# One decoder block with 32 experts: TensorE's order of work within an expert, and when the selection table is made

## The chip, the cores and the metric

One core of a Trainium2 chip runs the whole block in one program. The metric is the device time of one execution in microseconds (us); of several runs the median counts.

## The reference, cut to what matters

The program computes one decoder layer for 256 tokens of width 1024: a state-space branch and an attention branch over projections of the normalised input, a cross-attention into 256 memory tokens, a mixture of experts and a last normalisation. The change lies in the mixture of experts. Each token goes to 4 of 32 experts:

```python
logits = hf @ w_router + b_router
top_v, top_i = lax.top_k(logits, TOP_K)          # TOP_K = 4 of 32
gate = jax.nn.softmax(top_v, axis=-1)
# for the tokens xb of expert e:
gu = xb @ w_gu[e] + b_gu[e]                      # (tokens, 2048)
g_lin = jnp.minimum(gu[..., :D_FF], 7.0)
u_lin = jnp.clip(gu[..., D_FF:], -7.0, 7.0)
act = g_lin * jax.nn.sigmoid(1.702 * g_lin) * (u_lin + 1.0)
yb = act @ w_down[e] + b_down[e]                 # D_FF = 1024
y[token] += gate * yb
```

All is float32. The experts' weights are 32 x (8 MB + 4 MB).

## The kernel before, in words

Every engine has an instruction list of its own, written out by hand, and semaphores order the lists against one another. A `wait_ge(sem, n)` in a list stops that engine's queue until the semaphore is at n; what stands behind it waits too. The first part (to about 393 us) is the two branches, the cross-attention and the router. Then come the experts, in the function `experts` of each engine: a loop of 4 turns (`Fori(0, NIT)`) over a body of 8 experts (`BODY`), written out. The experts are taken in groups of 4 (`GE`), with 64 token slots an expert (`SLOTS`). If an expert had more than 64 tokens, further passes would run; here none does.

**Weights.** SP (L369 to L388) issues the transfers: for each expert 8 chunks of 1 MB of `w_gu` and 4 of `w_down` (`EXP_CH` = 12), into a ring of 16 slots (`RING_MOE`; 12 in `ring`, the rest in the buffers `small`, `xn`, `gates` and `kv`, free by then). SP issues chunk m when TensorE has used chunk m - 16, which the semaphore `chunk_used` counts. TensorE waits for a chunk on `slot_full`. This wait and the ring are the only thing that paces the transfers.

**One expert on TensorE** (L798 to L849), in this order:
- bias (L809): four 32-row products of the selection table `sel` (32 partitions, 4 experts x 64 slots, ones in the row of the expert) with `b_gu`, which open the sums in PSUM banks 4 and 5;
- gate/up (L818): 8 chunks x 4 products onto the same banks, `chunk_used` after each chunk;
- combine (L794): the down products of the expert before, copied by VectorE to `yb`, are added into banks 0 to 3 at their tokens through the table `hotT`; it waits for `yb_ready`;
- gather (L768): a quarter of the tokens of the next group of four experts is picked with the one-hot table `onehot`, into bank 7. After four experts the next group's tokens are all there (`xgT`, two buffers);
- transposes of this expert's gate table (L827, into bank 6), and, when VectorE has taken the gathered block (`gather_out`) and made the activation (`act_ready`), of the activation (L834, into bank 7);
- down (L845), when ScalarE has copied both transposes out (`ht_out`, `at_out`): 4 chunks, onto bank 6.

A product of a 64-slot expert is written twice, for the two halves of its columns, into the upper and lower 64 partitions of a bank. Each instruction of this float32 form shows twice in the trace.

**One expert on VectorE** (L1425 to L1462): minimum and clip of gate and up (L1448, L1449, the second sets `gu_read`), two products for the activation (L1452, L1456, `act_ready`), taking the gathered block (L1404 in `take_gathered`, `gather_out`), copying the down products to `yb` (L1462, `yb_ready`). At every fourth expert (`j % GE == 0`) VectorE does ahead of this: the gate table of the group (L1434, two instructions), `sel` for the group (L1441; it waits until the gate/up products of the expert before are done), and the one-hot for the next group (L1396 in `next_onehot`, `hot_ready`). **ScalarE** (L1066 to L1074): the sigmoid, and the two copies out of PSUM.

At a group's start TensorE waits ahead of the bias products for `hot_ready`:

```python
if j % GE == 0:
    pe.wait_ge(hot_ready, it * 2 + (j // GE + 2))
    pe.wait_ge(gather_out, it * 8 + (4 * (j // GE) + 4))
```

That `sel` is ready is told by `hot_ready`, since VectorE makes the one-hot after it.

Of the kernel before, what the change touches and what calls it, by code (L numbers as in the profile page):

```python
# [27 lines left out]
KD = D // P  # L28
# [8 lines left out]
NE, TOPK, FF = 32, 4, 1024  # L37
# [15 lines left out]
SLOTS = 64  # L53
GE = 4
# [5 lines left out]
EXP_CH = KD + FF // P // 2  # L60
# [30 lines left out]
FRONT_CH = len(CHUNKS)  # L91
# [48 lines left out]
STEP_CH = BODY * EXP_CH  # L140
# [18 lines left out]
def build(nc, x, mem, g_mix, w_in, conv_w, conv_b, dt_bias, a_log, d_skip, g_ssd, w_ssd_out,  # L159
# [5 lines left out]
    with ctx:  # L165
# [40 lines left out]
        identx = sb("identx", [NE, TABW])  # L206
# [56 lines left out]
        bgu = xcf[0:NE, 0:2 * FF]  # L263
# [15 lines left out]
        sel = scr[0:NE, 3, 0:GE * SLOTS].rearrange("p (e s) -> p e s", e=GE)  # L279
# [3 lines left out]
        def ring_slot(m):  # L283
# [4 lines left out]
        ps = ctx.enter_context(nc.psum_tensor("ps", [P, 8, 512], F32))  # L288
# [34 lines left out]
        gl_ready, gu_read, sg_ready, act_ready = map(  # L323
            sem, ("gl_ready", "gu_read", "sg_ready", "act_ready"))
        ht_done, ht_out, at_done, at_out, yb_ready, comb_done, y_done, yb_last, up_ready, h_full, \
            gatehot_made = map(
            sem, ("ht_done", "ht_out", "at_done", "at_out", "yb_ready", "comb_done", "y_done",
                  "yb_last", "up_ready", "h_full", "gatehot_made"))
        dve_step, act_step = sem("dve_step"), sem("act_step")
        out_sem, out_ready = sem("out_sem"), sem("out_ready")  # L330

# [136 lines left out]
        def _(pe):  # L468
# [295 lines left out]
            def gather(k0, bank=7):  # L764

                for k in range(2):
                    for b in range(TB):
                        i = mm(ps[:, bank, k * T:(k + 1) * T], hn2[:, b, (k0 + k) * P:(k0 + k + 1) * P],  # L768
                               onehot[:, b, :, :].rearrange("p e s -> p (e s)"), start=(b == 0), stop=(b == 1))
                i.then_inc(gathered, 1)  # L770
# [16 lines left out]
            def combine(done=comb_done, each=False):  # L787
# [7 lines left out]
                               skip_group_check=True)  # L795
                i.then_inc(done, 1)

            def experts(it):  # L798


                for j in range(BODY):
                    n = it * BODY + j
                    xg = xgT[j // GE]
                    if j % GE == 0:
                        pe.wait_ge(hot_ready, it * 2 + (j // GE + 2))
                        pe.wait_ge(gather_out, it * 8 + (4 * (j // GE) + 4))
                    for q in range(2):
                        for half in range(2):
                            mm(ps[64 * half:64 * half + 64, 4 + q, :], sel[:, j % GE, :],  # L809
                               bgu[:, q * FF + half * 512:q * FF + half * 512 + 512],  # L810
                               start=True, stop=False, skip_group_check=True)
                    for k in range(KD):
                        m = FRONT_CH + j * EXP_CH + k
                        pe.wait_ge(slot_full[slot(m)], it * (16 * STEP_CH // RING_MOE) + filled(m))
                        w = ring_slot(m)
                        for q in range(2):
                            for half in range(2):
                                i = mm(ps[64 * half:64 * half + 64, 4 + q, :],  # L818
                                       xg[:, k, (j % GE) * SLOTS:(j % GE + 1) * SLOTS],
                                       w[:, q * FF + half * 512:q * FF + half * 512 + 512],  # L820
                                       start=False, stop=(k == KD - 1), skip_group_check=True)
                        i.then_inc(chunk_used, 1)
                    pe.wait_ge(yb_ready, n + 1)
                    combine()
                    gather(2 * (j % GE))
                    for b in range(TB):
                        i = nc.tensor.transpose(ps[:, 6, b * P:(b + 1) * P],  # L827
                                                gatehot[:, b, j % GE].rearrange("p u s -> p (u s)"),
                                                ident[:])
                    i.then_inc(ht_done, 1)  # L830
                    pe.wait_ge(gather_out, it * 8 + (j + 5))
                    pe.wait_ge(act_ready, n + 1)
                    for c in range(4):
                        i = nc.tensor.transpose(ps[:, 7, c * P:(c + 1) * P], actv[:, c * P:(c + 1) * P], ident[:])  # L834
                    i.then_inc(at_done, 1)
                    pe.wait_ge(ht_out, n + 1)
                    pe.wait_ge(at_out, n + 1)
                    for k in range(FF // P):
                        m = FRONT_CH + j * EXP_CH + KD + k // 2
                        if k % 2 == 0:  # L840
                            pe.wait_ge(slot_full[slot(m)], it * (16 * STEP_CH // RING_MOE) + filled(m))
                        w = ring_slot(m).rearrange("p (k n) -> p k n", k=2)
                        fh, c = k // 4, k % 4
                        for half in range(2):
                            i = mm(ps[64 * half:64 * half + 64, 6, :], actT[:, c, fh * 64:fh * 64 + 64],  # L845
                                   w[:, k % 2, half * 512:(half + 1) * 512],
                                   start=(k == 0), stop=(k == FF // P - 1), skip_group_check=True)
                        if k % 2:
                            i.then_inc(chunk_used, 1)  # L849
# [239 lines left out]
        def _(dve):  # L1089
            V = nc.vector  # L1090
            count = [0]

            def step(ins):

                count[0] += 1
                ins.then_inc(dve_step, 1)
                dve.wait_ge(dve_step, count[0])
# [304 lines left out]
            def take_gathered(buf, k0, bank=7):  # L1402
                g = pcol[:, ROW_MOE + k0:ROW_MOE + k0 + 2].unsqueeze(2).broadcast_to([P, 2, T])
                V.tensor_tensor(buf[:, k0:k0 + 2, :], ps[:, bank, :].rearrange("p (k s) -> p k s", k=2), g,  # L1404
                                ALU.mult).then_inc(gather_out, 1)
# [7 lines left out]
            for p_ in range(NPASS):  # L1413
# [2 lines left out]
                    step(V.tensor_scalar(rankx[:, :, c], r0, -float(SLOTS * p_), None, ALU.add))  # L1416
                step(V.tensor_copy(gatex[:, :, c], gate_d[:]))

            step(V.memset(hotT, 0.0))
            V.memset(yb, 0.0).then_inc(yb_ready, 1)  # L1420
            for k0 in range(0, KD, 2):
# [3 lines left out]
            def experts(it):  # L1425
                for j in range(BODY):
                    n = it * BODY + j
                    if j % GE == 0:
                        gr = it * 2 + j // GE


                        dve.wait_ge(hot_ready, it * 2 + (j // GE + 1))
                        for b in range(TB):
                            i = V.tensor_tensor(gatehot[:, b],  # L1434
                                            onehot[:, b].unsqueeze(2).broadcast_to([P, GE, 2, SLOTS]),
                                            gatex[:, b, bass.ds(gr * GE, GE)].unsqueeze(2).unsqueeze(2)
                                            .broadcast_to([P, GE, 2, SLOTS]), ALU.mult)
                        i.then_inc(gatehot_made, 1)

                        dve.wait_ge(chunk_used, it * STEP_CH + (FRONT_CH + (j - 1) * EXP_CH + KD))  # L1440
                        V.tensor_copy(sel, identx[:, bass.ds(gr * GE, GE)].unsqueeze(2).broadcast_to([NE, GE, SLOTS]))  # L1441

                        dve.wait_ge(gathered, it * 8 + (j + 4))
                        dve.wait_ge(gatehot_made, it * 2 + (j // GE + 1))
                        next_onehot(gr * GE + GE, hot_ready)

                    dve.wait_ge(chunk_used, it * STEP_CH + (FRONT_CH + j * EXP_CH + KD))
                    V.tensor_scalar(gl, ps[:, 4, :], LIM, None, ALU.min).then_inc(gl_ready, 1)  # L1448
                    V.tensor_scalar(ul, ps[:, 5, :], LIM, -LIM, ALU.min, ALU.max).then_inc(gu_read, 1)  # L1449
                    dve.wait_ge(gl_ready, n + 1)  # L1450
                    dve.wait_ge(gu_read, n + 1)
                    V.scalar_tensor_tensor(out=ul, in0=ul, scalar=1.0, in1=gl, op0=ALU.add,  # L1452
                                           op1=ALU.mult).then_inc(up_ready, 1)
                    dve.wait_ge(up_ready, n + 1)
                    dve.wait_ge(sg_ready, n + 1)
                    V.tensor_tensor(actv, ul, sg, ALU.mult).then_inc(act_ready, 1)  # L1456
                    dve.wait_ge(gathered, it * 8 + (j + 5))
                    take_gathered(xgT[1 - j // GE], 2 * (j % GE))

                    dve.wait_ge(chunk_used, it * STEP_CH + (FRONT_CH + (j + 1) * EXP_CH))  # L1460
                    dve.wait_ge(comb_done, n + 1)
                    V.tensor_copy(yb, ps[:, 6, :]).then_inc(yb_ready, 1)  # L1462
# [42 lines left out]
```

## Time and profile before

| | us |
|---|---|
| median of three runs | 1387.34 |
| the three runs | 1392.22, 1387.34, 1384.44 |
| span of the profiled execution | 1386.0 |
| TensorE busy in the span | 1264.7 (91%) |
| VectorE busy | 310.8 (22%) |
| ScalarE busy | 190.1 (14%) |
| GpSimd busy | 119.1 (9%) |
| read from HBM | 450 MB, 325 GB/s over the span |

The profile is of one execution; its page gives the span from the first to the last instruction and no other time of that execution. The median of the runs is 1.3 us above the span. Matmuls are pipelined and their ends are modelled, so a busy TensorE isn't one at its peak. "PEclk" is the clock that TensorE was granted: 1.00 is 2.4 GHz and 0.50 is 1.2 GHz.

### The profile page before, as it was taken

How to read it: one execution, taken by the hardware profiler on the slowest of the kernel's cores; microseconds unless marked ns; L12 is line 12 of the kernel's file. 1: busy time of each engine (PE TensorE's matmuls, PEld its weight loads, DVE VectorE, ACT ScalarE, POOL GpSimd, SP SyncE). 2: the span in 40 equal slices, each digit the busy share in tenths (PEclk: the TensorE clock that was granted, in tenths of full speed). 3: DMA queues.
4: the chain of work that ended last, by engine and by line, in shares of the span. 5: the costliest groups of instructions: out<-in, count | busy, mean ns of one | idle time of the engine just before them, and what ended most of it. 6: DMA issues, size and time to landing. Idle time of an engine off the chain costs nothing.

```text
span 1386.0 us, 14515 instructions
## 1 busy us (share of the span) xinstructions
PE 1264.7 (91%) x5731; PEld 605.8 (44%) x5731; DVE 310.8 (22%) x439; ACT 190.1 (14%) x264; POOL 119.1 (9%) x64
## 2 busy tenths in 40 slices
PE   5988989999789998998999899899989989998996
PEld 5986766556453333333333333333333333333332
DVE  3926262213231111111111111112111111211112
ACT  3553562002100000000000000000000000000000
POOL 5655540000000000000000000000000000000000
PEclk9999999999869999999999999999999999999999
DMA  6433434900759999999999999999999999999980
GB/s 221 152 122 122 153 114 138 350 0 1 283 229 397 418 416 416 417 417 416 411 417 416 416 417 417 418 416 417 416 411 418 417 416 416 417 416 410 418 333 31
DMA packets 95385, 452.16 MB, mean 326 GB/s; under 512 B 7093, under 2 KB 7257, under 8 KB 62505
## 3 DMA queue, kind: packets, MB, share of 16 engines
q1 hardware_dynamic: 94584, 448.87, 80.7%
q0 software_dynamic: 720, 2.20, 0.6%
q8 instruction: 53, 0.87, 0.3%
q14 instruction: 28, 0.22, 0.0%
HBM read 450.00 MB, written 1.05 MB: 325 GB/s over the span
## 4 chain that ended last, share of the span: by engine, by line
PE 85%; DVE 8%; issue 3%; ACT 2%; POOL 1%; DMA 0%; DVEq 0%; POOLq 0%; ACTq 0%
PE ps L818 33%; PE ps L845 16%; PE ps L521 11%; PE ps L768 5%; PE ps L809 5%; PE ps L794 5%; PE ps L510 4%; DVE xcT L1146 3%; PE ps L834 2%; PE ps L536 1%; DVE nT L1404 1%; DVE xs L1404 1%; POOL w_lo L340 1%; DVE scr L1434 1%; PE ps L606 1%
## 5 line engine op out<-in xcount | busy, mean ns | idle before, releaser
L845 PE MATMUL ps<-ring,xbuf 128*64 128x512 f32 x768 | 170.1, 595 | 18.7 <-issue 11.7
L818 PE MATMUL ps<-ring,nT 128*64 128x512 f32 x768 | 168.1, 594 | 0.0
L818 PE MATMUL ps<-ring,xs 128*64 128x512 f32 x768 | 168.1, 594 | 0.0
L1448 DVE TENSOR_SCALAR xbuf<-ps 128x512 f32<-128x512 f32 x32 | 22.1, 691 | 509.8 <-PE ps L818 509.8
L1070 ACT ACTIVATE xbuf<-xbuf 128x512 f32<-128x512 f32 x32 | 20.1, 629 | 802.1 <-DVE xbuf L1448 802.1
L340 POOL TENSOR_TENSOR w_lo<-ring,w_hi 128x2048 fp32r<-128x2048 f32 x22 | 103.4, 4704 | 82.3 <-ACT w_hi L891 82.2
L845 PEld LDWEIGHTS ps<-ring,xbuf 128*64 128x64 f32 x768 | 60.6, 137 | 112.8 <-issue 112.8
L818 PEld LDWEIGHTS ps<-ring,nT 128*64 128x64 f32 x768 | 54.0, 137 | 112.6 <-issue 112.6
L818 PEld LDWEIGHTS ps<-ring,xs 128*64 128x64 f32 x768 | 53.9, 137 | 112.7 <-issue 112.7
L409 POOL TENSOR_SCALAR ss<-ss 128x2 f32<-128x2 f32 (+1 forms) x6 | 1.1, 189 | 1117.4 <-DVE ss L1101 1110.8
L809 PE MATMUL ps<-xcT,scr 32*64 32x512 f32 x256 | 65.8, 632 | 21.2 <-DVE scr L1396 21.2
L1462 DVE COPY xbuf<-ps 128x512 f32<-128x512 f32 x32 | 22.1, 691 | 275.4 <-PE ps L845 275.4
L768 PE MATMUL ps<-scr,gates 128*128 128x256 f32 x288 | 72.7, 398 | 1.0 <-DVE scr L1396 1.0
L794 PE MATMUL ps<-xbuf,scr 64*128 64x512 f32 x264 | 65.6, 615 | 2.5 <-DVE cnt_f L1472 2.5
L768 PEld LDWEIGHTS ps<-scr,gates 128*128 128x128 f32 x288 | 53.2, 194 | 32.0 <-issue 24.3
L510 PE MATMUL ps<-xT_hi,w_hi 128*128 128x256 f32 x160 | 48.2, 301 | 8.5 <-DVE w_lo L340 5.5
L521 PE MATMUL ps<-ring,nT 128*128 128x512 f32 x128 | 55.5, 593 | 0.1
L891 ACT ACTIVATE w_hi<-ring 128x2048 fp32r<-128x2048 f32 x24 | 45.7, 1909 | 52.2 <-PE ps L510 26.9
L510 PE MATMUL ps<-xT_hi,w_lo 128*128 128x256 f32 x160 | 47.8, 298 | 0.0
L510 PE MATMUL ps<-xT_lo,w_hi 128*128 128x256 f32 x160 | 47.5, 297 | 0.0
L521 PE MATMUL ps<-w_hi,xT_hi 128*128 128x512 f32 x112 | 47.4, 423 | 0.0
L809 PEld LDWEIGHTS ps<-xcT,scr 32*64 32x64 f32 x256 | 15.3, 132 | 66.6 <-issue 51.2
(272 smaller groups left out, 1322.9 us busy)
## 6 DMA issues: line engine op xcount, KB each, us to landing
ring<-in_w_gu SPq DMA_DIRECT2D x192, 1024.0 KB, 13.0
ring<-in_w_down SPq DMA_DIRECT2D x96, 1024.0 KB, 16.2
ring<-in_w_in SPq DMA_DIRECT2D x24, 1024.0 KB, 5.2
small<-in_w_gu SPq DMA_DIRECT2D x16, 1024.0 KB, 10.3
xn<-in_w_gu SPq DMA_DIRECT2D x16, 1024.0 KB, 11.0
gates<-in_w_gu SPq DMA_DIRECT2D x16, 1024.0 KB, 12.0
kv<-in_w_gu SPq DMA_DIRECT2D x16, 1024.0 KB, 12.8
small<-in_w_down SPq DMA_DIRECT2D x8, 1024.0 KB, 13.8
```

Of the source, the lines that this page charges most:

```text
L340: ops.tensor_tensor(w_lo[:, m % SPLIT, :], ring_slot(m), w_hi[:, m % SPLIT, :], ALU.subtract).then_inc(lo_ready[name], 1)
L510: i = mm(ps[:, b0 + cb // 2, (cb % 2) * T:(cb % 2 + 1) * T], w[:, k, cb * P:(cb + 1) * P], a[:, 4 * c + k, :], start=(c == 0 and k == 0 an ...
L521: i = mm(ps[:, b0 + b, :], a[:, 4 * c + k, b * P:(b + 1) * P], w[:, k, :], start=(c == 0 and k == 0 and q == 0), stop=(4 * c + k == STRIPE ...
L768: i = mm(ps[:, bank, k * T:(k + 1) * T], hn2[:, b, (k0 + k) * P:(k0 + k + 1) * P], onehot[:, b, :, :].rearrange("p e s -> p (e s)"), start ...
L794: i = mm(ps[:, 2 * b + half, :], hotT[r, b, :], yb[r, :], start=False, stop=False, skip_group_check=True)
L809: mm(ps[64 * half:64 * half + 64, 4 + q, :], sel[:, j % GE, :], bgu[:, q * FF + half * 512:q * FF + half * 512 + 512], start=True, stop=Fa ...
L818: i = mm(ps[64 * half:64 * half + 64, 4 + q, :], xg[:, k, (j % GE) * SLOTS:(j % GE + 1) * SLOTS], w[:, q * FF + half * 512:q * FF + half * ...
L834: i = nc.tensor.transpose(ps[:, 7, c * P:(c + 1) * P], actv[:, c * P:(c + 1) * P], ident[:])
L845: i = mm(ps[64 * half:64 * half + 64, 6, :], actT[:, c, fh * 64:fh * 64 + 64], w[:, k % 2, half * 512:(half + 1) * 512], start=(k == 0), s ...
L891: af(w_hi[:, m % SPLIT, :], ring_slot(m), ACT.Copy).then_inc(hi_ready, 1)
L1146: i = V.scalar_tensor_tensor(out=xcT[:, c, :], in0=xpad[:, c, tap:tap + T], scalar=pcol[:, ROW_CW + tap * NCB + c:ROW_CW + tap * NCB + c + 1],
L1404: V.tensor_tensor(buf[:, k0:k0 + 2, :], ps[:, bank, :].rearrange("p (k s) -> p k s", k=2), g, ALU.mult).then_inc(gather_out, 1)
```

## The change

The order on TensorE becomes gate/up, gather, combine, transposes of gate table and activation, bias products of the next expert, down. The first expert's bias products stand ahead of the loop. The wait for `hot_ready` moves behind the gate/up products. A new semaphore, `sel_ready`, tells that `sel` is ready: VectorE makes `sel` once ahead of the loop and then at every fourth expert (`j % GE == 3`) behind the taking of the gathered block. TensorE waits for it ahead of the bias products of a new group, and for `gu_read` ahead of all bias products of the loop, since VectorE must have read banks 4 and 5.

```diff
@@ TensorE
+            def bias(e):
+
+                for q in range(2):
+                    for half in range(2):
+                        mm(ps[64 * half:64 * half + 64, 4 + q, :], sel[:, e, :],
+                           bgu[:, q * FF + half * 512:q * FF + half * 512 + 512],
+                           start=True, stop=False, skip_group_check=True)
+
+            pe.wait_ge(sel_ready, 1)
+            bias(0)
+
             def experts(it):
-
 
                 for j in range(BODY):
                     n = it * BODY + j
                     xg = xgT[j // GE]
                     if j % GE == 0:
-                        pe.wait_ge(hot_ready, it * 2 + (j // GE + 2))
                         pe.wait_ge(gather_out, it * 8 + (4 * (j // GE) + 4))
-                    for q in range(2):
-                        for half in range(2):
-                            mm(ps[64 * half:64 * half + 64, 4 + q, :], sel[:, j % GE, :],
-                               bgu[:, q * FF + half * 512:q * FF + half * 512 + 512],
-                               start=True, stop=False, skip_group_check=True)
                     for k in range(KD):
...
                         i.then_inc(chunk_used, 1)
+                    if j % GE == 0:
+                        pe.wait_ge(hot_ready, it * 2 + (j // GE + 2))
+                    gather(2 * (j % GE))
                     pe.wait_ge(yb_ready, n + 1)
                     combine()
-                    gather(2 * (j % GE))
                     for b in range(TB):
                         i = nc.tensor.transpose(ps[:, 6, b * P:(b + 1) * P],
...
                         i = nc.tensor.transpose(ps[:, 7, c * P:(c + 1) * P], actv[:, c * P:(c + 1) * P], ident[:])
                     i.then_inc(at_done, 1)
+
+                    if j % GE == GE - 1:
+                        pe.wait_ge(sel_ready, it * 2 + (j // GE + 2))
+                    pe.wait_ge(gu_read, n + 1)
+                    bias((j + 1) % GE)
                     pe.wait_ge(ht_out, n + 1)
                     pe.wait_ge(at_out, n + 1)
@@ VectorE
+            def next_sel(col):
+
+                V.tensor_copy(sel, identx[:, bass.ds(col, GE)].unsqueeze(2)
+                              .broadcast_to([NE, GE, SLOTS])).then_inc(sel_ready, 1)
+
+            next_sel(0)
             step(V.memset(hotT, 0.0))
...
                         i.then_inc(gatehot_made, 1)
-
-                        dve.wait_ge(chunk_used, it * STEP_CH + (FRONT_CH + (j - 1) * EXP_CH + KD))
-                        V.tensor_copy(sel, identx[:, bass.ds(gr * GE, GE)].unsqueeze(2).broadcast_to([NE, GE, SLOTS]))
 
                         dve.wait_ge(gathered, it * 8 + (j + 4))
...
                     take_gathered(xgT[1 - j // GE], 2 * (j % GE))
+                    if j % GE == GE - 1:
+                        next_sel((it * 2 + (j // GE + 1)) * GE)
 
                     dve.wait_ge(chunk_used, it * STEP_CH + (FRONT_CH + (j + 1) * EXP_CH))
```

## Rows read from the trace of the kernel before

**Rows 1.** The page, the span in 40 slices: TensorE's granted clock and the DMA engines

```profile
PEclk9999999999869999999999999999999999999999
DMA  6433434900759999999999999999999999999980
```

**Rows 2.** The chain of waits, in order of time (start us, us, what)

```profile
408.16 16.75 PE ps L818 x64
...
467.00 1.86 PE ps L809 x8
468.87 13.88 PE ps L818 x64
...
1255.90 16.14 PE ps L818 x64
...
1344.84 13.88 PE ps L818 x64
...
1364.73 7.10 PE ps L845 x32
```

**Rows 3.** Timeline of TensorE, an expert's end (start us, us, line, operation, tiles, count [idle before])

```profile
874.12 1.99 PE L794 MATMUL ps<-xbuf,scr 64*128 64x512 f32 x8
876.03 1.99 PE L768 MATMUL ps<-scr,gates 128*128 128x256 f32 x8
877.86 0.38 PE L827 MATMUL ps<-ident,scr 128*128 128x128 f32 x2
878.81 0.66 PE L834 MATMUL ps<-ident,xbuf 128*128 128x128 f32 x4 [0.57 <-DVE xs L1404]
880.20 7.09 PE L845 MATMUL ps<-ring,xbuf 128*64 128x512 f32 x32 [0.73 <-issue]
```

**Rows 4.** Windows: us, five engines' busy time (instructions), clock, DMA share, GB/s

```profile
415.80:1342.50 926.70, 864.15 (x3878) 321.70 (x3874) 140.28 (x220) 53.74 (x96) 0.00 (x0) 0.98 1.02 415
1345.00:1351.70 6.70, 6.70 (x34) 2.17 (x32) 0.00 (x0) 0.00 (x0) 0.00 (x0) 1.00 0.10 40
```

**Rows 5.** Timeline of SP's queue: three chunk issues

```profile
433.05 0.35 SPq L378 DMA_DIRECT2D ring<-in_w_gu  x1
...
1323.18 0.33 SPq L378 DMA_DIRECT2D ring<-in_w_gu  x1
...
1330.05 2.66 SPq L383 DMA_DIRECT2D ring<-in_w_down  x1
```

**Rows 6.** DMA issues of the same three (KB each, us to landing)

```profile
ring<-in_w_gu SPq DMA_DIRECT2D x1, 1024.0 KB, 5.8
...
ring<-in_w_gu SPq DMA_DIRECT2D x1, 1024.0 KB, 17.8
...
ring<-in_w_down SPq DMA_DIRECT2D x1, 1024.0 KB, 21.6
```

**Rows 7.** Timeline of VectorE in the same expert as rows 3

```profile
876.35 0.69 DVE L1456 TENSOR_TENSOR xbuf<-xbuf 128x512 f32<-128x512 f32 x1
878.06 0.69 DVE L1404 TENSOR_TENSOR xs<-ps,pcol 128x512 f32<-128x512 f32 x1 [1.02 <-PE ps L768]
```

**Rows 8.** Timeline of VectorE and TensorE at the group boundary that follows

```profile
889.20 0.27 DVE L1441 COPY scr<-identx 32x256 f32 x1
...
890.39 2.35 PE L809 MATMUL ps<-xcT,scr 32*64 32x512 f32 x8 [3.10 <-DVE scr L1396]
```

**Rows 9.** Waits, longest in total: engine, tile, line, releaser: us in total, times, longest

```profile
PE ps L809 <- DVE scr L1396: 21.2, 7, 3.1
```

**Rows 10.** Windows (columns as rows 4) ahead of the first expert and at the boundary

```profile
403.70:407.10 3.40, 3.40 (x12) 1.03 (x12) 1.38 (x4) 0.00 (x0) 0.00 (x0) 1.00 0.00 0
407.10:413.90 6.80, 6.80 (x18) 1.72 (x16) 0.00 (x0) 0.00 (x0) 0.00 (x0) 0.50 0.12 27
...
888.40:891.80 3.40, 1.41 (x8) 0.48 (x8) 1.83 (x5) 0.00 (x0) 0.00 (x0) 1.00 1.04 424
891.80:895.20 3.40, 3.40 (x10) 0.77 (x8) 0.00 (x0) 0.00 (x0) 0.00 (x0) 0.50 1.01 413
```

More of the change, by code:

```diff
@@ L325, in build @@
         ht_done, ht_out, at_done, at_out, yb_ready, comb_done, y_done, yb_last, up_ready, h_full, \
-            gatehot_made = map(
+            gatehot_made, sel_ready = map(
             sem, ("ht_done", "ht_out", "at_done", "at_out", "yb_ready", "comb_done", "y_done",
-                  "yb_last", "up_ready", "h_full", "gatehot_made"))
+                  "yb_last", "up_ready", "h_full", "gatehot_made",
+                  "sel_ready"))
         dve_step, act_step = sem("dve_step"), sem("act_step")
```

## The prediction

> **What bounds the kernel now.** I began with the slices of the page [rows 1]: from the twelfth slice to the last but one the DMA row reads 9 while TensorE is given its full clock. So two resources look full, and the question is which one the other waits for. The chain of waits answers for today: from 408 to 1371.8 us it is TensorE's own work plus short waits for VectorE or ScalarE, and never a transfer. Four experts take (1255.90 - 408.16) / 7 = 121.1 us [rows 2], an ordinary one 28.85 us: bias products 1.86, gate/up products 13.88, then 6.0 from the first combine product to the first down product (874.12 to 880.20 less modelled ends) and 7.09 of down products [rows 2, 3]. Four times 28.85 is 115.4, so each of the seven group boundaries costs 5.7 us more.
>
> Then the transfers. The windows put the 16 DMA engines at a share of 1.02 and 415 GB/s from 415.8 to 1342.5 us [rows 4]: they are never without work, though SP issues each 1 MB chunk only when TensorE has given up a slot. The issue times and times to landing [rows 5, 6] tell how much is in stock. The first gate/up chunk of the third expert is issued at 433.05, lands 5.8 later, at 438.9, and is used from 468.87 [rows 2]: 30 us of stock. The last gate/up chunk of the last expert is issued at 1323.18, lands 17.8 later, at 1341.0, and is used in the last eighth of the products that start at 1344.84, at 1357.0: 16 us of stock. The last chunk of all, issued at 1330.05, lands at 1351.7. So 359 chunks land in 1351.7 - 438.9 = 912.8 us, 2.543 us each, 30.5 us for an expert's twelve, against TensorE's mean of 30.3. **The transfers are slightly slower than TensorE already, and live on a stock that is half used up at the end.** They finish when the slowest DMA engine does: from 1345.0 to 1351.7 the rate is 40 GB/s, about a tenth of full [rows 4], one or two engines finishing alone.
>
> **The change, part by part.** TensorE's instructions are the same ones, and so are VectorE's but for one early copy.
> (1) Gather ahead of combine. Today the gather ends near 878.04; VectorE had finished the activation product at 877.04 and stood idle 1.02, then spends 0.69 in taking the gathered block, and TensorE waits 0.57 before the activation transposes [rows 3, 7]. With the gather 1.92 earlier VectorE takes the block straight after 877.04 and is done near 877.75, while TensorE is busy with combine and the gate transposes to 878.24. The 0.57 is gone: 32 x 0.57 = 18 us of TensorE. Combine reads the table and yb of the expert before, long ready; it costs nothing there; were yb late, it would wait for one copy of that size, 0.69 [rows 7].
> (2) The next bias between the transposes and down. Today TensorE waits 0.73 for ScalarE's copy of the transposes [rows 3]. Now 1.86 of bias products lies there and covers it: 32 x 0.73 = 23 us. The new wait for gu_read is for VectorE's read of banks 4 and 5, which comes ahead of the activation product and so is over 1.8 us old when the transposes end; behind it in TensorE's queue stand bias and down, so if VectorE were late both would be.
> (3) No wait for VectorE at a boundary. Today VectorE copies yb when the down products end at 887.3, makes the gate table, then the selection table (0.27, from 889.20) and the one-hot, and TensorE starts bias at 890.39 after 3.10 idle [rows 8]; such a wait occurs 7 times, 21.2 us [rows 9]. Behind it the clock is at half from 891.80 to 895.20 [rows 10], and the gate/up products take 16.75 or 16.14 instead of 13.88 [rows 2]. Both go: the one-hot is now needed only behind 13.88 us of gate/up products, which cover VectorE's 3 us. That is the 5.7 of above, 7 x 5.7 = 40 us.
> (4) The selection copy, 0.27, moved behind the taking of the gathered block, ends near 878.05; its bias starts at 878.9. Nothing, and 0.27 at most if VectorE runs late. At the loop's head it is one copy more on VectorE ahead of work that TensorE's 32 gather products hide: zero. SP's and POOL's queues get no new instruction, and no DMA is moved.
> TensorE's side thus gains 18 + 23 + 40 = 81 us: 27.5 us an expert, an end of the down products near 1291.
>
> **But the chunks don't come faster.** With 27.5 against 30.5 the stock of 30 us is used up at 3.0 an expert, after ten experts or so, near 720 us. From then on TensorE waits for chunks and the transfers, which were without a break before and stay so, set the end. Their first issue waits on the first gate/up chunk, whose start (bias behind the gateT products, clock at half) I see nothing to move. So the last gate/up chunk still lands at 1341.0. From there: last products 13.88/8 = 1.73 to 1342.7; gather, combine and both transposes, 5.35 less the 0.57 wait, 4.8; bias 1.86; down 7.09, for which the last chunk, landed at 1351.7, is early enough (wanted at 1354.7): 1356.5. Behind the down products come 1386.0 - 1371.8 = 14.2 us of untouched work [rows 2]: **a span of 1370.7**. The forecast adds the 1.3 by which the median of the runs, 1387.34, stands above the span of 1386.0: **1372 us**. So of 81 us some 15 arrive; the rest becomes waiting for data.
>
> The unknown of this sum is the pace of the transfers when more of them are outstanding, which no row of the kernel before shows over more than 21.6 us of queue. From below: the mean rate of 415 instead of the slowest engine's (359 MB in 912.8 us is 412 GB/s) would bring the last landing 7 us forward. From above: 1% slower would cost 9 us. The pace was the same while times to landing grew from 5.8 to 21.6 us, so I take no change. The Trainium skill, page "DMA: Bandwidth & Descriptors", section "Bandwidth", has 425 GB/s for a 16 MB transfer; this trace shows 412 to 415, and by the page's figure, an estimate, the last landing would come 27 us earlier and the median near 1345.
>
> **The rivals.** *A, slower: the clock falls in every expert.* The change puts combine (64 rows), transposes and bias (32 rows, 1.86) side by side. For it: from 403.7 to 407.1 TensorE was busy throughout, with 32-row products only, and directly after it, before the first gate/up products, had half its clock, so that these took 16.75 [rows 2, 10]. Against it: in an ordinary expert the 1.86 of bias stood between 128-row products, and the gate/up products behind it still took 13.88 [rows 2]; in the new order transposes ahead of it and down products behind it have 128 rows again. Price: a half-clock stretch of 3.4 us loses 1.7, one of 6.8 loses 3.4 (at boundaries the gate/up products took 2.9 and 2.3 more [rows 2]). It decides from a loss of 3.0 an expert on; below that it is hidden under the transfers. At 3.4: 30.9 x 32 = 989, down ends at 1397, median about 1413. The clock may also fall where TensorE waits for chunks: that is 30.5 - 27.5 = 3.0 us an expert, split over its last two or three gate/up chunks, beside 1.73 of products each; at one fall an expert it would add some 2 us at the end and no more, since TensorE has those 3 us to spare. The Trainium skill, page "TensorE: Matmul & The Clock Gate", section "HAM oscillation", tells of a kernel whose waits for data threw it back to half clock again and again, which speaks against this change; no row of before has a wait for data.
> *B, no difference:* the deeper queue makes the slowest engine slower by 1.7% or more; 16 us later, all is hidden, 1387.
> *C, much faster:* the limit is not the DMA engines but the few chunks asked for at a time, and with up to 16 outstanding the pace is the best that a short stretch shows, 424 GB/s [rows 10]. Against it is the share of 1.02. The 359 chunks, 376.4 MB, then take 888 us instead of 913: 25 us less, a median near 1347. This is the outcome that the Trainium skill's figure for large transfers, named above, would bring too.
> *D, the change doesn't do all it says:* the waits of 0.57 and 0.73 stay, being delays of any order. TensorE is still rid of the boundaries' 5.7; at 28.85 an expert it gains 1.66 on the transfers' 30.5, has used up 30 us of stock after 18 experts of 32, and the end is the same 1372. So most ways of being wrong about TensorE don't move the number.
>
> **How the numbers follow.** Transfers set the end (with D): 0.78, from 1364 (the mean rate) to 1381 (1% slower) but for 0.01. C or a pace between: 0.08. B: 0.08. A: 0.06. The range leaves out C, B's far end and A: 1362 to 1381. About 0.5% (7 us) is what a measurement can tell here, so faster means below 1380.4: 0.85; same 0.08; slower 0.07.
>
> **What would show it.** Right: DMA share stays at 1.0 to 1345 us and the last landing stays near 1352; median time to landing rises from 13 to over 25 us; TensorE has new waits in front of gate/up products after about 720 us and none before L834 or the down products; the bias products follow the transposes with no wait; an expert before 720 us takes 27.5, after it 30.5. Wrong: half-clock stretches in most experts (A); GB/s above 418 (C); a last landing after 1360 (B).

## The result, and the profile after

The changed kernel takes 1372.26 us (median of four runs, 1370.05 to 1375.38) against 1386.95 before (1384.44 to 1392.22); the ratio is 0.990, with a 95% interval of 0.987 to 0.992. The profiled execution has a span of 1370.1 us, predicted were 1370.7, and a time of 1371.97. The forecast was 1372.

The page of the changed kernel, the slices that answer to [rows 1], and the first line of the chain, in shares of the span:

```profile
PEclk9899989999969999999999999999999999999999
DMA  6433424900569999999999999999999999999992
...
PE 46%; SPq 28%; DMA 16%; issue 3%; DVE 3%; ACT 1%; POOL 1%; DVEq 0%; POOLq 0%; ACTq 0%
```

The slices look as before, and TensorE is as busy as before. What changed is the chain: it was TensorE's own work all through the experts, and now 44% of the span (28 and 16) runs over SP's issues and the transfers. The chain of waits in order of time shows where it turns (start us, us, what), here an early expert and the last one:

```profile
437.00 13.73 PE ps L823 x64
450.74 1.93 PE ps L769 x8
452.66 1.92 PE ps L795 x8
455.38 1.86 PE ps L803 x8
457.25 7.02 PE ps L857 x32
464.26 13.73 PE ps L823 x64
...
1314.50 25.93 DMA ring<-in_w_gu
1340.47 1.94 PE ps L823 x8
1342.41 1.92 PE ps L769 x8
...
1347.06 1.86 PE ps L803 x8
1348.92 7.04 PE ps L857 x32
```

L823 is gate/up, L769 gather, L795 combine, L841 the activation's transposes, L803 bias and L857 down. An early expert takes 464.26 - 437.00 = 27.26 us with no wait in it, where [rows 2, 3] had 28.85. The last expert's last gate/up products start when their chunk has landed. TensorE's timeline in that expert, answering to [rows 3] (in brackets the idle time ahead):

```profile
1338.12 1.94 PE L823 MATMUL ps<-ring,nT 128*64 128x512 f32 x8 [1.32 <-DMA ring<-in_w_gu]
1340.47 1.94 PE L823 MATMUL ps<-ring,nT 128*64 128x512 f32 x8 [0.41 <-DMA ring<-in_w_gu]
...
1346.46 0.60 PE L841 MATMUL ps<-ident,xbuf 128*128 128x128 f32 x4
1346.99 1.93 PE L803 MATMUL ps<-xcT,scr 32*64 32x512 f32 x8
1348.85 7.09 PE L857 MATMUL ps<-ring,xbuf 128*64 128x512 f32 x32
```

From the transposes to the down products no bracket is left: the 0.57 and the 0.73 are gone. The brackets stand ahead of the gate/up products instead. TensorE's waits over the whole span, in total, times and longest:

```profile
PE ps L823 <- DMA ring<-in_w_gu: 33.6, 65, 1.3
...
PE ps L823 <- issue: 7.3, 3, 2.6
PE ps L823 <- DMA gates<-in_w_gu: 2.8, 5, 0.6
PE ps L823 <- DMA kv<-in_w_gu: 2.8, 5, 0.6
...
PE ps L823 <- DMA xn<-in_w_gu: 2.7, 5, 0.5
...
PE ps L823 <- DMA small<-in_w_gu: 1.9, 4, 0.6
```

That is 43.8 us in 84 waits for chunks, and a chunk's products behind such a wait show 1.94 instead of 13.73/8 = 1.72, another 0.22 x 84 = 18. The 21.2 us of [rows 9] don't occur any more. And the transfers, in windows (columns as [rows 4]) and by the first and last issue:

```profile
415.80:1342.50 926.70, 875.70 (x3943) 306.57 (x3940) 138.15 (x222) 53.79 (x96) 0.00 (x0) 1.00 1.01 415
...
1345.00:1352.00 7.00, 7.00 (x36) 2.45 (x34) 1.06 (x3) 0.98 (x2) 0.00 (x0) 1.00 0.05 21
```

```profile
411.15 0.33 SPq L379 DMA_DIRECT2D small<-in_w_gu  x1
...
1328.15 4.11 SPq L384 DMA_DIRECT2D ring<-in_w_down  x1
```

```profile
ring<-in_w_down SPq DMA_DIRECT2D x1, 1024.0 KB, 23.0
```

The same 415 GB/s, and the last chunk lands at 1328.15 + 23.0 = 1351.1; before it was 1351.7 [rows 5, 6]. **The profiled end of the kernel moved by 16 us and the end of the transfers by half a microsecond.**

SP's queue looks like a third candidate for the bound, with its 28% of the chain. The issue of a `w_down` chunk took 0.38 us in the kernel before and takes 4.1 now, one of `w_gu` 0.33 and now 1.0 (medians from 1100 to 1330 us). From SP's timeline, one issue before and four in the changed kernel:

```profile
1295.91 0.38 SPq L383 DMA_DIRECT2D small<-in_w_down  x1
...
1315.77 16.49 SPq L384 DMA_DIRECT2D ring<-in_w_down  x4
```

SP's queue is taken up by its issues for 19% of that stretch before and 90% now, and yet the chunks land at the same pace. So SP is held back and doesn't set the pace. Between 700 and 1340 us it waits 458 us for used slots in the kernel before and not at all in the changed one.

### The profile page after: what moved, and what is told of

It reads as the page before. It is cut to its first block, busy times and chain, and to the rows that moved or that the text cites. A ratio compares the mean times of both kernels' runs of the same rounds, so it can differ in the third digit from the quotient of the medians.

```text
span 1370.1 us, 14536 instructions
## 1 busy us (share of the span) xinstructions
PE 1263.9 (92%) x5739; PEld 587.5 (43%) x5739; DVE 308.2 (22%) x440; ACT 190.2 (14%) x264; POOL 119.5 (9%) x64
## 4 chain that ended last, share of the span: by engine, by line
PE 46%; SPq 28%; DMA 16%; issue 3%; DVE 3%; ACT 1%; POOL 1%; DVEq 0%; POOLq 0%; ACTq 0%
SPq L379 14%; SPq L384 14%; PE ps L823 11%; PE ps L522 11%; DMA ring<-in_w_gu 11%; PE ps L511 6%; PE ps L857 6%; DMA xn<-in_w_gu 3%; PE ps L769 2%; DMA gates<-in_w_gu 2%; PE ps L803 2%; PE ps L795 2%; PE ps L537 1%; PE ps L552 1%; POOL w_lo L341 1%
## 5 line engine op out<-in xcount | busy, mean ns | idle before, releaser
L823 PE MATMUL ps<-ring,nT 128*64 128x512 f32 x768 | 175.6, 597 | 20.6 <-DMA ring<-in_w_gu 20.6
L823 PE MATMUL ps<-ring,xs 128*64 128x512 f32 x768 | 173.3, 596 | 13.0 <-DMA ring<-in_w_gu 13.0
L857 PE MATMUL ps<-ring,xbuf 128*64 128x512 f32 x768 | 170.1, 595 | 0.0
L823 PEld LDWEIGHTS ps<-ring,nT 128*64 128x64 f32 x768 | 51.6, 136 | 142.4 <-issue 83.1
L823 PEld LDWEIGHTS ps<-ring,xs 128*64 128x64 f32 x768 | 52.8, 137 | 130.8 <-issue 90.3
L857 PEld LDWEIGHTS ps<-ring,xbuf 128*64 128x64 f32 x768 | 52.9, 137 | 115.5 <-issue 115.5
L769 PE MATMUL ps<-scr,gates 128*128 128x256 f32 x288 | 73.8, 403 | 1.0 <-DVE scr L1408 1.0
L769 PEld LDWEIGHTS ps<-scr,gates 128*128 128x128 f32 x288 | 54.0, 197 | 34.0 <-issue 26.0
L795 PE MATMUL ps<-xbuf,scr 64*128 64x512 f32 x264 | 65.6, 615 | 2.5 <-DVE cnt_f L1489 2.5
L803 PE MATMUL ps<-xcT,scr 32*64 32x512 f32 x264 | 63.8, 600 | 0.0
L522 PE MATMUL ps<-w_hi,xT_lo 128*128 128x512 f32 x112 | 44.0, 393 | 0.0
## 6 DMA issues: line engine op xcount, KB each, us to landing
ring<-in_w_gu SPq DMA_DIRECT2D x192, 1024.0 KB, 20.9
ring<-in_w_down SPq DMA_DIRECT2D x96, 1024.0 KB, 25.9
small<-in_w_down SPq DMA_DIRECT2D x8, 1024.0 KB, 25.9
```

The costliest lines, as they stand in the source:

```text
L522: i = mm(ps[:, b0 + b, :], a[:, 4 * c + k, b * P:(b + 1) * P], w[:, k, :], start=(c == 0 and k == 0 and q == 0), stop=(4 * c + k == STRIPE ...
L795: i = mm(ps[:, 2 * b + half, :], hotT[r, b, :], yb[r, :], start=False, stop=False, skip_group_check=True)
L803: mm(ps[64 * half:64 * half + 64, 4 + q, :], sel[:, e, :], bgu[:, q * FF + half * 512:q * FF + half * 512 + 512], start=True, stop=False, ...
L823: i = mm(ps[64 * half:64 * half + 64, 4 + q, :], xg[:, k, (j % GE) * SLOTS:(j % GE + 1) * SLOTS], w[:, q * FF + half * 512:q * FF + half * ...
```

## Experiments

Twelve kernels ran, each timed in turn with the kernel before on the same chip (its median there 1385.7 to 1387.6). Theory T is the prediction's: the transfers set the end of the changed kernel, TensorE that of the kernel before.

### Fewer bytes, the same instructions

The `w_down` transfers halved, in both kernels, whose down products use the half that came twice and leave out the other half of the weights (lines shortened):

```diff
-    src = w_down[0, bass.ds(g * BODY + j, 1), r:r + 2 * P, :]
-    sp_.dma_start(ring_slot(m).rearrange("p (k n) -> p k n", k=2),
-                  src.rearrange("e (k p) n -> p (e k) n", p=P))
+    src = w_down[0, bass.ds(g * BODY + j, 1), r:r + P, :]
+    sp_.dma_start(ring_slot(m)[:, 0:D], src.rearrange("e p n -> (e p) n"))
...
-    w[:, k % 2, half * 512:(half + 1) * 512]
+    w[:, 0, half * 512:(half + 1) * 512]
```

> The changed kernel with only the first half of each w_down chunk transferred (512 KB instead of 1 MB, both rows of products taken from it; the down products leave out half of the weights). TensorE's instructions are the same, the bytes fall by a sixth, from 30.5 to about 25.5 us of transfers an expert. Theory T (transfers set the end of the changed kernel, TensorE's gain is hidden): TensorE becomes the bound at its 27.3 us an expert, all 81 us of its gain show: median near 1307, no waits for data. Rival R (TensorE still sets the end, and the change gave it only some 15 us): median stays near 1372, within 5.

> The same halving of the w_down transfers in the kernel before (the down products leave out half of the weights). Theory T: there TensorE is the bound and nothing moves: 1387, within 4. If the transfers had already bounded the kernel before: some 20 to 60 us less.

Measured: the changed kernel 1307.9 us (1306.1 to 1313.0), ratio to before 0.944 (0.942 to 0.946); the kernel before 1387.4, ratio 1.000 (0.999 to 1.001). TensorE's only waits left in the experts of the first of them, from 440 us on:

```profile
PE ps L821 <- issue: 5.9, 3, 2.2
```

A sixth of the bytes less moves the kernel before by nothing and the changed one by 64 us, down to what TensorE needs: the prediction had its down products end at 1291, which with 14.2 and 1.3 behind them is 1306.5. The changed kernel's waits, 43.8 + 18 = 62 us, are near those 64. This settles what bounds each kernel, and that the change did give TensorE its 80 us.

### More TensorE work, the same bytes

The bias products twice, in the changed kernel

```diff
-                    bias((j + 1) % GE)
+                    for _ in range(2):
+                        bias((j + 1) % GE)
```

and in the kernel before (`for q in [0, 1] * 2`).

> The changed kernel with every bias product of the loop done twice (it opens its sum anew, so the result is the same): 1.86 us more TensorE work an expert, 60 us in all, 29.1 instead of 27.3 an expert, still under the transfers' 30.5. Theory T: only the last expert's path from the last gate/up chunk to the down products grows: 1.9 more, median near 1374, and the waits for gate/up chunks shrink by about the same 1.86 an expert where they are. Rival R: 1432.

> The same doubling of the bias products in the kernel before. Theory T: TensorE is the bound there, and the 32 times 1.86 show almost whole: 1387 + 60 = 1447, less what a longer stretch of the boundary's half clock adds or takes, 1440 to 1460; the stock of landed chunks grows instead of shrinking, time to landing falls to about 5 us. If the kernel before had been bound by transfers: under 1400.

Measured: 1406.9 us (1405.7 to 1410.0), ratio 1.014 (1.013 to 1.016), and 1468.9 (1466.5 to 1472.1), ratio 1.058 (1.057 to 1.060). Both missed, e3 by 33 us and e4 by 9 beyond its interval. Two experts from its chain, and its clock in a window that covers the second's down products (columns as [rows 10]):

```profile
518.82 4.11 PE ps L803 x16
522.92 9.83 PE ps L858 x32
...
551.14 3.58 PE ps L803 x16
554.72 7.02 PE ps L858 x32
```

```profile
521.70:528.50 6.80, 6.80 (x18) 1.71 (x16) 0.00 (x0) 0.00 (x0) 0.00 (x0) 0.50 1.02 387
```

Behind the doubled bias products the clock is at half and the down products take 9.83 instead of 7.02. From 414 to 1340 us the trace's record of the clock has 18 such stretches with 88 us together, every one behind the doubled bias products, where the changed kernel has 2 with 7 us: (88 - 7) / 2 = 41 us of work lost, on top of 60. TensorE was the bound again, with no wait for a chunk after 440. From the other side, e1's 1307.9 (no such stretch up to 1280 us) + 60 + 88 / 2 = 1412, 5 above the measured time. In e4 it was 85 us at half clock against 34 in the kernel before, 26 lost, and 1387 + 60 + 26 = 1473 is near the measured 1469 (the time to landing of its `w_gu` chunks fell to 8.1 us, not to 5). So e3 didn't test what it was made for, but showed rival A's mechanism at twice its dose. Two kernels with the same amount of extra work, placed or made otherwise, were to tell the clock from the work:

```diff
                         if k % 2:
                             i.then_inc(chunk_used, 1)
+                    bias((j + 1) % GE)
```

> The changed kernel with every bias product done twice like e3, but the second time behind the down products, not directly behind the first. TensorE has the same 60 us more of work, 29.1 us an expert, yet no stretch of 32-row products longer than 1.86. Theory K (e3 came out at 1407 instead of 1374 because the 3.7 us in a row of 32-row products, behind the transposes, lost TensorE its clock in 18 experts): here the clock holds but for a few falls, the work is hidden under the transfers, median 1372 to 1374. Rival L (the work itself is not hidden: 29.1 with its waits is as much as the transfers take): 1395 or more, as in e3.

```diff
+                    gather(2 * (j % GE), done=False)
                     gather(2 * (j % GE))
```

> The changed kernel with every gather of the loop done twice (the sum is opened anew, the result is the same): 1.93 us more TensorE work an expert as in e3 and e9, of 128-row products. Theory T and K: hidden but for the last expert's 1.9, median about 1374, no more falls of the clock than in the changed kernel. Rival L: 1400 or more.

Measured: e9 1372.7 us (1369.4 to 1375.0), ratio 0.990 (0.987 to 0.993); e12 1379.2 (1374.2 to 1379.8), ratio 0.993 (0.991 to 0.996). **60 us of additional TensorE work cost nothing in e9**; its waits for gate/up chunks after 600 us had shrunk to

```profile
PE ps L823 <- issue: 5.5, 3, 1.9
PE ps L823 <- DMA ring<-in_w_gu: 1.8, 4, 0.6
```

Theory K stands, L falls: the same 32-row products, the same number of them, lose the clock in 18 experts when 3.6 us of them stand in a row behind the transposes, and in none when they stand apart (the one fall of e9 after 414 us is behind a turn of the loop). e12 came out 5 above its 1374. Ahead of its first expert TensorE did this:

```profile
402.44 4.52 PE L786 MATMUL ps<-xcT,gateT 32*128 32x512 f32 x8
406.88 3.68 PE L804 MATMUL ps<-xcT,scr 32*64 32x512 f32 x8
410.49 3.68 PE L824 MATMUL ps<-small,xs 128*64 128x512 f32 x8
```

where the changed kernel did this:

```profile
402.34 3.69 PE L785 MATMUL ps<-xcT,gateT 32*128 32x512 f32 x8
405.96 1.93 PE L803 MATMUL ps<-xcT,scr 32*64 32x512 f32 x8
407.83 3.15 PE L823 MATMUL ps<-small,xs 128*64 128x512 f32 x8
```

The half clock ahead of the first expert (407.1 to 413.9 in [rows 10]) caught 10 us in e12's execution and 3.4 in the changed kernel's. So the first chunk was used, and the first transfer issued, 3.2 us later, and the last one landed 4.1 later. With the 1.9 that was expected this makes 6.0 of the 7.2 us by which the two profiled spans differ. It is read from one execution of each, and not shown for the other runs. Across the profiled executions (us; the last landing is the last issue plus its time to landing):

| | first issue | last landing | difference |
|---|---|---|---|
| before | 411.95 | 1351.65 | 939.7 |
| changed | 411.15 | 1351.15 | 940.0 |
| e5 | 411.09 | 1349.78 | 938.7 |
| e6 | 410.89 | 1350.69 | 939.8 |
| e9 | 411.53 | 1352.30 | 940.8 |
| e12 | 414.35 | 1355.22 | 940.9 |
| e7, 8 KB rows | 412.01 | 1344.36 | 932.3 |
| e10, 8 KB rows | 413.80 | 1346.62 | 932.8 |

In these runs the stream of 368 chunks lasts 939 to 941 us, whether the median time from issue to landing of a `w_gu` chunk is 13.0 us (before) or 20.9 (changed); only its start and its layout move it. Where TensorE is slow enough it stretches the stream, since it frees the slots: 948.1 us in e3 and 1005.9 in e4.

### Parts of the change

The swap of gather and combine alone, on the kernel before, and the changed kernel without the swap:

```diff
-                    pe.wait_ge(yb_ready, n + 1)
-                    combine()
                     gather(2 * (j % GE))
+                    pe.wait_ge(yb_ready, n + 1)
+                    combine()
```

> The kernel before with only gather put ahead of combine; bias, selection table and the boundary wait stay. It takes the 0.57 us wait ahead of the activation transposes away, 18 us of TensorE in all, against a stock of 16 us that the kernel before has left at its last gate/up chunk. Theory T: the stock is used up just at the end, and the whole gain of the change is there already: 1370 to 1374, the rest of the change worth nothing on top. Rival S (the 15 us of the full change come mainly from the boundary waits, and a wait of 0.57 only moves to the next semaphore): 1385 or more.

> The changed kernel with combine ahead of gather again, as before; bias ahead of down and the selection table made early stay. TensorE then takes 27.3 + 0.57 = 27.9 us an expert, under 30.5. Theory T: 1372, at most 1 more. Rival S: all parts count, 1372 + 18 = 1390.

Measured: e5 1373.4 us (1370.8 to 1376.3), ratio 0.991 (0.989 to 0.993); e6 1373.7 (1372.2 to 1376.3), ratio 0.992 (0.990 to 0.993). Either part alone has the whole gain (e6 came out 0.7 above the 1373 that it was allowed, less than its runs differ by). They are not bound alike, though. e5's waits over the span still hold the boundary, and none for a chunk; e6's hold chunks:

```profile
PE ps L809 <- DVE scr L1396: 21.1, 7, 3.1
PE ps L845 <- ACT scr L1072: 17.6, 24, 0.7
```

```profile
PE ps L823 <- DMA ring<-in_w_gu: 18.6, 33, 1.3
```

In e5 the last expert's gate/up products end at 1344.1 without a wait, their last chunk was needed at 1342.4 and had landed at 1339.0. Of the 16 us of stock that the kernel before ended with, the swap took 13. e5 is TensorE-bound to the end and misses the transfers by 3 us; that it ties with the full change is a match of sizes, as its expectation said. The swap took 13 and not its 18 also because TensorE had 48 us at half clock from 414 to 1340 us, against 34 in the kernel before.

e6 shows something else that its time hides. In seven of its experts the clock falls directly behind the single block of bias products, in one more behind a turn of the loop. The first of them (columns as [rows 10]):

```profile
513.90:517.30 3.40, 3.40 (x10) 1.00 (x10) 0.00 (x0) 0.00 (x0) 0.00 (x0) 0.50 1.01 410
```

The only difference from the changed kernel, which has no such fall, is that combine stands ahead of gather and the wait of 0.57 us is back ahead of the activation's transposes; which of the two it is, no run tells. Seven stretches of 3.4 us cost 12 us of TensorE, hidden under the transfers. All four runs of e6 have a mean clock of 0.967 to 0.969, those of the changed kernel 0.973 to 0.975.

### A faster stream

Each partition gets two neighbouring rows of `w_down`, 8 KB in one piece instead of two of 4 KB; the transposes take every other column to match:

```diff
-    src.rearrange("e (k p) n -> p (e k) n", p=P)
+    src.rearrange("e (p k) n -> p (e k) n", k=2)
...
-    actv[:, c * P:(c + 1) * P]
+    actv[:, c // 2 * 256 + c % 2:c // 2 * 256 + c % 2 + 255:2]
```

> The changed kernel with each w_down chunk laid so that a partition gets two neighbouring rows, 8 KB in one piece as for w_gu instead of two pieces of 4 KB; the activation transposes take every other column to match, the result is the same. In the trace of before the w_down chunks land 2.56 us apart and the w_gu chunks 2.49, so an expert's four would gain 0.28 us, 32 experts 9 us. Theory T: the transfers set the end, so the median falls by about 9, to 1363 (1359 to 1367). Rival R: no effect, or a loss if strided transposes are slower.

> The same layout of w_down in the kernel before. Theory T: TensorE is the bound, no effect: 1387, within 4, with more stock at the end (last chunk landed some 9 us earlier than at 1351.7).

Measured: e7 1366.1 us (1364.6 to 1366.9), ratio 0.985 (0.984 to 0.987); e8 1393.0 (1390.5 to 1397.4), ratio 1.004 (1.003 to 1.006). The page's rates by slice, changed kernel and e7:

```profile
GB/s 223 154 124 123 154 92 134 367 17 0 215 276 376 420 418 416 415 416 417 418 417 417 417 416 416 416 418 417 418 416 417 416 416 418 418 417 417 415 416 106
```

```profile
GB/s 224 155 124 123 154 93 135 371 14 0 213 280 344 423 421 421 420 421 420 422 421 421 421 422 421 420 420 421 422 421 421 420 420 421 421 422 421 421 415 81
```

From some 417 to 421: the stream is 7.7 us shorter (table) and the kernel 6 us faster. The same edit makes the kernel before slower, and e8 missed its interval by 2 us. TensorE's timeline in the second expert, of e8 and then of the kernel before:

```profile
462.83 0.74 PE L834 MATMUL ps<-ident,xbuf 128*128 128x128 f32 x4 [0.56 <-DVE nT L1404]
464.45 1.94 PE L845 MATMUL ps<-ring,xbuf 128*64 128x512 f32 x8 [0.87 <-ACT xbuf L1074]
...
459.92 7.09 PE L845 MATMUL ps<-ring,xbuf 128*64 128x512 f32 x32 [0.87 <-ACT xbuf L1074]
```

The strided transposes take 0.74 instead of the 0.66 of [rows 3]. The wait behind them is no longer than before: that expert has 0.87 in both kernels. An ordinary expert takes 28.93 us instead of 28.85, so 0.08 to 0.09 x 32 = 3 us of TensorE are paid where TensorE is the bound and hidden where it is not. e8 lost 7.3 (1393.0 against 1385.7 beside it), so more than half of the loss is open. The clock has a part in the profiled execution: 37 us at half clock from 414 to 1340 us against 34, and a first gate/up product at 412.86 instead of 408.09, with half clock ahead of it. Whether that belongs to the edit, no run tells. My expectation for e8 had left the transposes out, and put the last landing at about 1343. It came at 1353.0, with a first issue 4.8 us later than before (416.71 against 411.95) and a stream of 936.3 us. The rest of the change is worth something only with the faster stream:

> The swap alone (e5) with the w_down layout of e7. e5 had the whole gain of the change already. Theory T: with the transfers 7 us faster TensorE becomes the bound again, and the strided transposes cost it some 7 us as in e8: about 1376 to 1380, some 10 above e7, which is what the rest of the change is worth once the transfers are faster. If the rest of the change is worth nothing in any case: 1366.

Measured: 1375.6 us (1374.5 to 1380.8), ratio 0.992 (0.990 to 0.995): 9.4 above e7 as expected, and 0.4 below the interval. That interval had 7 us for the transposes; with 3 it is 1373.4 + 3 = 1376.4.

> The kernel of e7 with the first expert's bias products put between the second and the third gather ahead of the loop, so that only 3.6 us of 32-row products stand before the first gate/up products, not 5.5. The transfers stand still there since the ring is full, until the first chunk is used. Theory T: if the clock then holds, the first chunks are used 1.7 us earlier, the stream of transfers and so the end with them: 1364 to 1365 against the 1366.1 of e7. If it falls all the same, or the transfers' start does not count: 1366.

```diff
             for k0 in range(0, KD, 2):
+                if k0 == 4:
+                    pe.wait_ge(gt_out, 1)
+                    pe.wait_ge(rk_ready, 1)
+                    pe.wait_ge(moe_in, 32)
+                    pe.wait_ge(sel_ready, 1)
+                    bias(0)
...
-            pe.wait_ge(sel_ready, 1)
-            bias(0)
```

Measured: 1363.1 us (1360.5 to 1368.3), ratio 0.983 (0.981 to 0.986), the lowest median of all. Its five runs spread wider than e7's and enclose them, and in the profiled one, its slowest (1368.3), the clock fell before the first expert all the same and the first issue came at 413.8, later than e7's. Whether the early bias helps is open. The 8 KB rows are shown to beat both kernels, by e7 already (0.984 to 0.987 of the kernel before, where the changed one has 0.987 to 0.992).

## Why the prediction was right, point by point

**The two sides and their stock.** Predicted were TensorE ahead of the transfers by 3.0 us an expert (27.5 against 30.5) and the stock gone after ten experts, near 720. The early expert takes 27.26, and the first run of waits for chunks begins at 719.96; up to 700 us there is one single wait, of 0.6.

**The four parts.** (1) and (2): both waits are gone, in every expert. (3): the wait for VectorE is gone, but the boundary isn't free everywhere. Three times, at the turns of the loop of 8 experts, TensorE stands still for 2.2 to 2.6 us with no releaser shown (the 7.3 us of waits for "issue"), and behind two of them the clock falls, as here:

```profile
1114.29 3.05 PE L823 MATMUL ps<-small,xs 128*64 128x512 f32 x8 [2.61 <-issue]
```

```profile
1114.90:1118.30 3.40, 3.40 (x12) 1.02 (x9) 0.00 (x0) 0.00 (x0) 0.00 (x0) 0.51 1.01 414
```

The prediction had not seen that the 3.10 of [rows 8] covered a loop turn as well. 7 us of TensorE and some 3 of clock were thus over-counted in its 81. That e1 measured 80 all the same is partly luck: the ordinary expert, 27.26 instead of 27.5, gave 0.24 x 32 = 8 us more than predicted. (4) cost nothing.

**The sum from the last gate/up chunk.** Predicted start of its products 1341.0, seen 1340.47; end of the down products 1356.5, seen 1348.92 + 7.04 = 1355.96; behind them 14.2, seen 14.1. The transfers set the first of these and TensorE's path through one expert the rest. The median stands 2.2 above the profiled span instead of 1.3, so that two errors of under a microsecond cancel: that the median fits to 0.3 us is luck, that the span fits to 0.6 is what the sum can claim.

**The unknown.** The pace with more chunks outstanding was taken as unchanged, and the table of streams shows it: 940.0 against 939.7. (The 7 us for the mean rate, below which the range went, are 5.8: 376.4 MB at 415 GB/s take 907.0 us instead of 912.8.) That one straggler sets the last landing can be read from the trace: of the sixteen updates that tell of the last chunk's landing fifteen came by 1345.5 us and the sixteenth at 1351.1, in the kernel before by 1346.7 and at 1351.6. The lag of the sixteenth grows along the changed kernel's stream, from 0.1 us in a chunk that lands at 590 to 4.7 in one at 1201. That the sixteenth is one DMA engine, as the prediction had it, fits but isn't named in the trace. The best short stretch of 424 GB/s (C) was no promise. What did quicken the stream is the size of the rows. The Trainium skill, page "DMA: Bandwidth & Descriptors", section "Bandwidth", gives 425 GB/s for a 16 MB transfer issued from GpSimd. Here, with 386 MB in one stream, no slice of the changed kernel is above 420 and none of e7 above 423, so the measured rate decides.

**The rivals.** A: the order with one bias block behind the transposes holds the clock (no fall behind bias products in the changed kernel's record after 414 us, both falls are behind loop turns); with two it falls in 18 of 32 experts (e3), and with one but combine ahead of gather in seven (e6). The margin was smaller than the prediction made it look, and the swap of gather and combine is a part of what kept it. The waits for chunks, of up to 1.3 us between 1.9 of products, made no fall. The Trainium skill, page "TensorE: Matmul & The Clock Gate", section "HAM oscillation", tells of waits for data that do; those were of 3 to 5 us each, and this trace has none so long. B, C: fell with the stream's length. D was not built as it stands, with both waits kept and the boundaries gone; e5 (the boundaries kept) and e6 (the 0.57 kept) show what it claimed, that a part of the change on TensorE's side gives the same time.

**One sign was off.** Time to landing was to rise from 13 to over 25 us. The page after:

```profile
ring<-in_w_gu SPq DMA_DIRECT2D x192, 1024.0 KB, 20.9
ring<-in_w_down SPq DMA_DIRECT2D x96, 1024.0 KB, 25.9
```

The rise came, less for the gate/up chunks. The prediction let SP issue a chunk as soon as TensorE had given up its slot, up to 16 outstanding. But the slot of the last chunk was free from 1311.6 on, when the gate/up products of the expert before ended, and its issue came at 1328.15, behind issues of 4.1 us each. At 2.55 us a chunk 20.9 and 25.9 us are 8 to 10 chunks on their way and not 16. What holds an issue back, the trace doesn't say.

## What to carry to other kernels

Two resources that both look full need one number each: the time that either would take alone, and the stock between them at the beginning and at the end. The gain of a faster engine is capped by the stock that is left at the end; here 16 of 81 us, which one line of the change had nearly used up. Then test the claim from both sides: take bytes away and add engine work, in both kernels, and mind that the added work is of a kind that leaves the clock alone.

## What the runs showed of the hardware that was not expected

- TensorE that is busy without a break can lose its clock by the kind of its work: 3.6 us of 32-row products behind transposes lost it in 18 of 32 experts (e3), the same products in two pieces did not (e9). One piece of 1.86 us behind a wait of 0.57 and the transposes lost it in seven (e6).
- `w_down` in 8 KB instead of 4 KB pieces, a third of the bytes, raised the steady rate from some 417 to 421 GB/s and shortened a stream of 940 us by 7.7 (e7).
- In the last 7 us of the stream little is still moved (40 GB/s before, 21 after, of 415), and one of sixteen landing updates comes 5 to 6 us behind the other fifteen (changed 1351.1 against 1345.5; before 1351.6 against 1346.7): this straggler, not the mean rate, sets the last landing.
- SP's issue of a 1 MB chunk took 0.33 to 0.38 us with a median of 13 us to landing (before), and 1.0 (`w_gu`, 8 KB rows) or 4.1 (`w_down`, 4 KB rows) with 21 and more (changed). The pace of the transfers was the same.
- A turn of the loop of 8 experts costs TensorE 1.7 to 2.6 us when nothing else hides it (changed kernel, e1, e3, e6, e7, e9, e10, e12); the clock fell behind none, one or two of a kernel's three turns.
- Activation transposes that read every other column take 0.74 instead of 0.66 us for four (e8).
